# Modulation vectors of a two-block transformer: from TensorE products to VectorE multiply-and-sum

## The chip, the cores and the metric

The kernel runs on one core of one Trainium2 chip. The metric is the device time of one execution in microseconds (us); lower is better. PE is TensorE, DVE VectorE, ACT ScalarE, POOL GpSimd and SP SyncE, whose only work here is to issue DMAs.

## What is computed

Two transformer blocks of two layers each run one after the other on 1024 tokens of width 1024, in float32. In every layer a conditioning vector gives shifts, scales and gates, the modulation vectors:

```python
# first block, per layer: w_mod is 1024 x 3072
mod = silu(c) @ w_mod[l] + b_mod[l]                 # 24 vectors of 128
# second block, per layer: w_ada is 1024 x 6144, used for tokens and for context
mod_x = silu(c_2) @ w_ada[l] + b_ada[l]             # 48 vectors of 128
mod_c = silu(c_ctx_2) @ w_ada[l] + b_ada[l]
sh1, sc1, g1, sh2, sc2, g2 = split(mod_x, 6)
x = x + g1 * rmsnorm(mixer(rmsnorm(x, g) * (1 + sc1) + sh1), g_post)
x = x + g2 * rmsnorm(square(relu(hx2 @ w1)) @ w2, g_ff)
```

In blocks of 128 outputs that is 2 x (24 + 48) = 144 pieces of weight, 128 x 1024 numbers (512 KB) each. The first block's mixer joins window attention, retention and gated linear attention (GLA); the second block's joins window attention, a spatial gate and a Fourier transform, and a feed-forward follows it.

## The kernel before

**Stages.** `load_and_modulate` loads constants, computes the first layer's first 16 pieces and the rotation tables (to 57 us of the span). The first block follows, to about 1213 us, and then the second block, to the end at 3957 us.

**First block.** Four units (two layers, two halves of 512 tokens: unit 0 to 3), 283.2 us apart. A unit has 32 chunks; a chunk is one 128-wide slice of outputs: SP loads its weights into `wraw` (two slots, `load`), ACT copies them to `whi` (float32r, a rounded form), POOL subtracts to get the rest `wlo` (`split_low`, two halves), and PE makes 24 matmuls of 512 columns (`high_products`: `h_hi` and `h_lo` by `whi`; `low_products`: `h_hi` by `wlo`). Each chunk s of the first 24 is divided into two half-steps `at` = 2s and 2s + 1, and at each half-step every engine does its part of the mixer (`mixers(it, at)`), written out in tables of numbers: GLA's decays are summed at `at` 5 (DVE, `log_sums`), its seven levels are scored at `at` 8, 9, 10, 11, 12, 14 and 16 (`LEVEL_AT`), its outputs come at 19 to 22, retention's at 23 to 27, rotations of q and k at 2c + 3 for nine chunks c (`ROPE_AT`: 11, 13, 19, 21, ..., 31), attention from 30 on. No scheduler moves anything: each engine takes its instructions in the order written.

**A level.** POOL makes a distance (`distance`, L540), ACT takes its exponent, POOL multiplies keys (`keys`, L551) and DVE queries (`queries`, L922), PE scores (`level`, L1243) into `quad`, and DVE picks the wanted entries out of `quad` (`pick`, L932). PE scores level n + 1 only when level n is picked.

**Modulation.** In four units the remaining 128 pieces are computed, four in a group, 8 groups a unit. PE multiplies at chunks s with s % 4 < 2 (`mod_step`, matmuls at L189, two pieces each, into `bankM`); DVE transposes `bankM` (`mod_rows`, L1052); PE folds (`fold_products`, L197) at the chunks of `FOLD_AT`; DVE adds the bias (`mod_columns`, four instructions at L204). `bankM` also takes four sums over heads per unit (`head_sum`), so each user waits for the one before. `mod_ring` has four slots; SP loads two pieces at s % 4 = 1 and two at s % 4 = 2 (`mod_loads`, L500), behind the chunk's weights and, after rotated chunks, behind `turned_half`, four small DMAs (L491) that wait until ACT has copied out the chunk just finished.

**Unit edges.** A unit's last chunk is followed by the next one's first: DVE scales x (`x_scaled`, L863), adds the last bias group (L204), makes `h_lo` (`x_low`, L871), and then, when the root of the last squares is there, adds y to x (`update`, L890 and L891) ahead of the new unit's mixers.

**Second block.** 64 chunks per feed-forward of 512 tokens, in four groups of eight `hidden` and eight `output` chunks. In `hidden` DVE squares (L2551) and makes `a_lo` (L2554); in `output` it adds to y (L2577). The last layer's columns are made in `project` (`columns2`).

Of the kernel before, what the change touches and what calls it, by code (L numbers as in the profile page):

```python
# [17 lines left out]
P = 128  # L18
# [31 lines left out]
FOLD_AT = [4 * g + (2 if g in (3, 4) else 3) for g in range(8)]  # L50
# [10 lines left out]
MOD_RING = 4  # L61
# [11 lines left out]
ROW_PAD = 896  # L73
# [135 lines left out]
def load_and_modulate(nc, t, a, sem):  # L209

    groups = MOD_FIRST // MOD_GROUP
    with ExitStack() as ctx:
# [3 lines left out]
        ring = sb("first_ring", [P, MOD_FIRST, D])  # L216
# [18 lines left out]
        def _(sp):  # L235
            sp.dma_start(cvec[:], a["c"]).then_inc(vec_in, 16)
            sp.dma_start(t["fold"][:], a["fold"]).then_inc(vec_in, 16)
# [6 lines left out]
            for m in range(MOD_RING):  # L244
                sp.dma_start(t["mod_ring"][:, m, :], a["w_mod"][MOD_FIRST + m]).then_inc(t["mod_in"][m], 16)
# [4 lines left out]
            sp.wait_ge(t["rope_saved"], 16 * 4 * NB)  # L250

        @block.scalar
        def _(act):
# [10 lines left out]
            nc.scalar.activation(t["cact"][:, :, 0:VEC], cvec[:], ACT.Silu).then_inc(cact_ready, 1)  # L264
# [10 lines left out]
        def _(pe):  # L275
            def to_columns(g):
                pe.wait_ge(row_ready, g + 1)
                at = 4 * VEC * MOD_GROUP
                fold_products(nc, psM[:, at * g:at * (g + 1)], t["fold"][:], row[:, g % 2, :]).then_inc(turned, 1)

            pe.wait_ge(cact_ready, 2)
            for g in range(groups):
# [3 lines left out]
                for c in range(MOD_GROUP):  # L286
                    mod_products(nc, psR[g % 2], c * P, t["cact"], ring, g * MOD_GROUP + c).then_inc(summed, 1)
# [5 lines left out]
        def _(dve):  # L293
# [23 lines left out]
            nc.vector.memset(t["cact"][:], 0.0).then_inc(cact_ready, 1)  # L317
# [50 lines left out]
def first_block(nc, t, a, sem):  # L368

    with ExitStack() as ctx:  # L370
# [6 lines left out]
        mods, mod_ring, cact = t["mods"], t["mod_ring"], t["cact"]  # L377
# [12 lines left out]
        mod_row = sb("mod_row", [P, MOD_GROUP * P])  # L390
# [63 lines left out]
        mod_summed, mod_row_ready, mod_turned, mod_out = sig("mod_summed", MOD_GROUP), sig("mod_row_out", 1), sig("mod_turned", 1), sig("mod_out", 1)  # L454
        mod_in = t["mod_in"]
        mod_groups = (MODS - MOD_FIRST) // MOD_GROUP // UNITS
# [13 lines left out]
        def group_of(it, s):  # L470

            return it * mod_groups + s // 4

        def mod_source(m):
            return a["w_mod"][m] if m < DEPTH * MOD1 else a["w_ada"][m - DEPTH * MOD1]

        @block.sync
        def _(sp):
# [14 lines left out]
            def mod_loads(it, s):  # L493

                g = group_of(it, s) + 1
                for c in range(2 * (s % 4) - 2, 2 * (s % 4)):
                    m = MOD_FIRST + MOD_GROUP * g + c
                    if m < MODS:
                        sp.wait_ge(*mod_summed.after(g - 1, c + 1))
                        sp.dma_start(mod_ring[:, c, :], mod_source(m)).then_inc(mod_in[c], 16)  # L500

            sp.dma_start(rope[:], t["rope_tables"][0]).then_inc(rope_in.sem, 16)
            for c in range(2):
                load(0, c)
            for it in range(UNITS):
                for s in range(CH1):
# [3 lines left out]
                    if s % 4 in (1, 2):  # L510
                        mod_loads(it, s)
# [338 lines left out]
        def _(dve):  # L850
# [195 lines left out]
            def mod_rows(it, s):  # L1046

                g = group_of(it, s)
                dve.wait_ge(*mod_summed.after(g, MOD_GROUP))
                if g:  # L1050
                    dve.wait_ge(*mod_turned.after(g - 1, 1))
                nc.vector.transpose(mod_row[:], bankM[:]).then_inc(*mod_row_ready.one)  # L1052

            def mod_columns(it, s):

                g = group_of(it, s)
                q = MOD_FIRST + MOD_GROUP * g
                dve.wait_ge(*mod_turned.after(g, 1))
                biased(nc, mods[:, q:q + MOD_GROUP, :], bankM[:, 0:4 * VEC * MOD_GROUP], t["mod_bias"][:, q:q + MOD_GROUP],
                       MOD_GROUP).then_inc(*mod_out.one)  # L1060
                dve.wait_ge(*mod_out.after(g, 1))
# [2139 lines left out]
```

## Time and profile before

| | |
|---|---|
| time, median of 3 runs | 3964.49 us (3963.75 to 3964.65) |
| the profiled execution | 3959.07 us, span 3957.3 us |
| busy: PE, PE weight loads | 93%, 75% |
| busy: DVE, ACT, POOL | 54%, 44%, 45% |
| granted PE clock, mean | 0.976 of full speed |
| HBM read, whole run | 397.40 MB |

The profiled execution is 5.4 us faster than the median; 1.8 us of it lie outside its span. Busy shares are over stages with different limits; which engine sets the end of a stage is read from that stage's own rows. `mod_ring<-in_w_ada` stands for a DMA into `mod_ring`, `lin<-h_hi,whi` for a matmul of those two into PSUM.

### The profile page before, as it was taken

How to read it: one execution, taken by the hardware profiler on the slowest of the kernel's cores; microseconds unless marked ns; L12 is line 12 of the kernel's file. 1: busy time of each engine (PE TensorE's matmuls, PEld its weight loads, DVE VectorE, ACT ScalarE, POOL GpSimd, SP SyncE). 2: the span in 40 equal slices, each digit the busy share in tenths (PEclk: the TensorE clock that was granted, in tenths of full speed). 3: DMA queues.
4: the chain of work that ended last, by engine and by line, in shares of the span. 5: the costliest groups of instructions: out<-in, count | busy, mean ns of one | idle time of the engine just before them, and what ended most of it. 6: DMA issues, size and time to landing. Idle time of an engine off the chain costs nothing.

```text
span 3957.3 us, 61376 instructions
## 1 busy us (share of the span) xinstructions
PE 3674.5 (93%) x22388; PEld 2983.7 (75%) x22388; DVE 2127.4 (54%) x3355; ACT 1725.4 (44%) x2899; POOL 1775.3 (45%) x1288
## 2 busy tenths in 40 slices
PE   4999999999997899888999999999899899999997
PEld 3867767777776777667888998887777778888886
DVE  5546556556456567667224655336567674335234
ACT  2355355355354544555324453335454553243233
POOL 1543444344443422325445885555322355455454
PEclk8999999999999999999999999999999999999999
DMA  6433433433433321112232453222221122233323
GB/s 251 132 127 123 150 120 129 136 134 134 132 111 109 111 74 52 56 59 88 95 99 95 150 170 108 96 96 82 97 70 54 64 80 96 90 96 97 97 94 104
DMA packets 127221, 421.32 MB, mean 106 GB/s; under 512 B 17280, under 2 KB 19104, under 8 KB 126368
## 3 DMA queue, kind: packets, MB, share of 16 engines
q1 hardware_dynamic: 121488, 410.09, 31.2%
q10 hardware_dynamic: 5520, 8.34, 0.6%
q8 instruction: 140, 2.29, 0.2%
q14 instruction: 73, 0.60, 0.0%
HBM read 397.40 MB, written 6.29 MB: 102 GB/s over the span
## 4 chain that ended last, share of the span: by engine, by line
PE 54%; DVE 8%; ACT 3%; issue 2%; POOL 0%; DMA 0%; SPq 0%; ACTq 0%; DVEq 0%; POOLq 0%
PE lin L2673 30%; PE lin L2682 15%; PE bankO L2798 2%; PE lin L2931 2%; PE bankT L2740 2%; DVE x L2318 1%; DVE tmp L2284 1%; DVE y L2317 1%; DVE staged L2296 1%; PE scores L2773 1%; DVE h_lo L2307 1%; ACT whi L1903 1%; PE lin L2815 1%; PE scores L2774 0%; PE lin L2703 0%
## 5 line engine op out<-in xcount | busy, mean ns | idle before, releaser
L1884 POOL TENSOR_TENSOR wlo<-late_raw,whi 128x512 fp32r<-128x512 f32 x456 | 641.5, 1431 | 750.6 <-PE lin L2682 489.8
L1884 POOL TENSOR_TENSOR wlo<-wraw,whi 128x512 fp32r<-128x512 f32 x452 | 635.1, 1428 | 703.5 <-PE lin L2682 485.8
L2673 PE MATMUL lin<-h_hi,whi 128*128 128x512 f32 (+1 forms) x1896 | 709.3, 381 | 48.1 <-ACT y_context L2197 13.8
L2673 PE MATMUL lin<-h_lo,whi 128*128 128x512 f32 (+1 forms) x1896 | 695.9, 374 | 0.0
L525 POOL TENSOR_TENSOR wlo<-wraw,whi 128x512 fp32r<-128x512 f32 x260 | 356.7, 1393 | 465.9 <-PE lin L1170 284.6
L2673 PE MATMUL lin<-a_hi,whi 128*128 128x512 f32 (+1 forms) x1280 | 465.7, 371 | 10.9 <-ACT tmp L2206 8.1
L2673 PEld LDWEIGHTS lin<-h_hi,whi 128*128 128x128 f32 x1896 | 364.2, 192 | 132.3 <-issue 24.3
L2673 PE MATMUL lin<-a_lo,whi 128*128 128x512 f32 (+1 forms) x1280 | 462.6, 369 | 0.0
L1903 ACT ACTIVATE whi<-late_raw 128x1024 fp32r<-128x1024 f32 x228 | 239.2, 1058 | 509.0 <-PE lin L2673 406.8
L1903 ACT ACTIVATE whi<-wraw 128x1024 fp32r<-128x1024 f32 x226 | 237.3, 1058 | 487.1 <-PE lin L2673 402.9
L2682 PE MATMUL lin<-h_hi,wlo 128*128 128x512 f32 (+1 forms) x1896 | 440.4, 375 | 1.2 <-POOL wlo L1884 0.8
L2673 PEld LDWEIGHTS lin<-h_lo,whi 128*128 128x128 f32 x1896 | 364.8, 192 | 60.2 <-issue 1.2
L2682 PEld LDWEIGHTS lin<-h_hi,wlo 128*128 128x128 f32 x1896 | 335.3, 191 | 64.8 <-issue 4.4
L2551 DVE TENSOR_TENSOR tmp<-tmp 128x512 f32<-128x512 f32 (+1 forms) x160 | 185.2, 1157 | 333.8 <-ACT tmp L2206 328.2
L1162 PE MATMUL lin<-h_hi,whi 128*128 128x512 f32 x800 | 333.4, 417 | 13.1 <-DVE h_lo L871 13.1
L1162 PE MATMUL lin<-h_lo,whi 128*128 128x512 f32 x800 | 322.1, 403 | 0.0
L2682 PE MATMUL lin<-a_hi,wlo 128*128 128x512 f32 (+1 forms) x1280 | 288.6, 370 | 2.3 <-POOL wlo L1884 2.3
L2673 PEld LDWEIGHTS lin<-a_hi,whi 128*128 128x128 f32 x1280 | 242.3, 189 | 59.3 <-ACT tmp L2206 15.7
L2673 PEld LDWEIGHTS lin<-a_lo,whi 128*128 128x128 f32 x1280 | 242.4, 189 | 39.7 <-issue 0.2
L2577 DVE TENSOR_TENSOR y<-lin,y 128x512 f32 (+1 forms) x96 | 66.4, 692 | 361.3 <-PE lin L2682 361.0
L2682 PEld LDWEIGHTS lin<-a_hi,wlo 128*128 128x128 f32 x1280 | 224.8, 188 | 44.9 <-POOL wlo L1884 3.5
L622 ACT ACTIVATE whi<-wraw 128x1024 fp32r<-128x1024 f32 x130 | 136.7, 1057 | 269.1 <-PE lin L1162 200.7
(382 smaller groups left out, 6429.8 us busy)
## 6 DMA issues: line engine op xcount, KB each, us to landing
wraw<-in_w SPq DMA_DIRECT2D x332, 512.0 KB, 3.5
late_raw<-in_w SPq DMA_DIRECT2D x212, 512.0 KB, 3.4
mod_ring<-in_w_ada SPq DMA_DIRECT2D x96, 512.0 KB, 4.5
mod_ring<-in_w_mod SPq DMA_DIRECT2D x32, 512.0 KB, 4.6
tmp<-tmp SPq DMA_DIRECT2D x224, 64.0 KB, 2.0
first_ring<-in_w_mod SPq DMA_DIRECT2D x16, 512.0 KB, 16.6
wraw<-in_dft_tokens SPq DMA_DIRECT2D x16, 512.0 KB, 3.5
late_raw<-in_dft_tokens SPq DMA_DIRECT2D x16, 512.0 KB, 3.5
```

What stands on the lines that cost most here:

```text
L525: last = nc.gpsimd.tensor_tensor(wlo[:, s, half], wraw[:, s, half], whi[:, s, half].bitcast(F32), ALU.subtract)
L622: nc.scalar.activation(whi[:, s, :], wraw[:, s, :], ACT.Copy).then_inc(*w_hi.one)
L1162: last = nc.tensor.matmul(bank[c % 2], whi[:, c % 2, k * P:(k + 1) * P], h[:, k, :], start=(k == 0 and h is h_hi), stop=False)
L1884: last = nc.gpsimd.tensor_tensor(wlo[:, s, half], raw_chunk[r][:, half], whi[:, s, half].bitcast(F32), ALU.subtract)
L1903: nc.scalar.activation(whi[:, s, 0:D], raw_chunk[r], ACT.Copy).then_inc(*w_hi.one)
L2551: nc.vector.tensor_tensor(tmp[:, 2 + s, 0:w], tmp[:, 4 + s, 0:w], tmp[:, 4 + s, 0:w], ALU.mult).then_inc(*a_sq.one)
L2577: nc.vector.tensor_tensor(part, bank[s][:, 0:p.w], part, ALU.add).then_inc(*lin_free.one)
L2673: last = nc.tensor.matmul(bank[s][:, 0:p.w], whi[:, s, k * P:(k + 1) * P], h[:, k, 0:p.w], start=(k == 0 and h is parts[0]), stop=False)
L2682: last = nc.tensor.matmul(bank[s][:, 0:p.w], wlo[:, s, k * P:(k + 1) * P], parts[0][:, k, 0:p.w], start=False, stop=(k == KB - 1))
L2740: last = nc.tensor.transpose(out, probs[i % 2][:, kv, k * P:(k + 1) * P], ident[:])
L2798: last = nc.tensor.matmul(bankO[half, g * P:(g + 1) * P], v, probsT[:, kv, at:at + P], start=(k == 0), stop=(k == n - 1))
L2931: return nc.tensor.matmul(bank[c][:, 0:2 * P].rearrange("p (t n) -> p t n", t=2), x_part[:, k, cols], w[:, 0:2, k * P:(k + 1) * P], start= ...
```

## The change

The pieces from 16 on are laid out by output (a row of 1024 weights for each of 128 outputs, the partitions), in `mod_rows`. silu(c) of the three vectors is written to HBM (`c_flat`), and copied from there to all partitions (`c_wide`). One DVE instruction (`tensor_tensor_reduce`) then multiplies a piece by a vector, adds up along the row on top of the bias, and leaves the sum in `mods`. PE's `mod_step`, the fold, `mod_rows` and `mod_columns` are gone from the first block, and `head_sum` no longer waits for them. `w_ada` pieces need two products (tokens, context). In the first block each unit has 32 products at the half-steps of `MOD_AT`: 32 pieces of `w_mod` in unit 0 (one product each), 48 of `w_ada` (layer 0) in units 1 to 3 (two each). The other 48, of the last layer, go into the first layer's feed-forwards of tokens, 48 products in each of two. `mod_ring` has two slots; a slot's next load is issued by SP when the last product on it is done.

```diff
-FOLD_AT = [4 * g + (2 if g in (3, 4) else 3) for g in range(8)]
+MOD_AT = list(range(3, 30)) + [31, 35, 39, 43, 46]
-MOD_RING = 4
+MOD_RING = 2
...
+                for c in range(MOD_RING, MOD_EARLY):
+                    done = products_through(c - MOD_RING)
+                    if ((done - 1) // UNIT_MODS, MOD_AT[(done - 1) % UNIT_MODS] // 2 + 1) == (it, s):
+                        sp.wait_ge(*mod_done.after(0, done))
+                        sp.dma_start(mod_ring[:, c % MOD_RING, :], a["mod_rows"][c]).then_inc(mod_in[c % MOD_RING], 16)
...
+            def modulation(e):
+                c, v = mod_product(e)
+                row = mod_ring[:, c % MOD_RING, :]
+                if v < 2:
+                    dve.wait_ge(mod_in[c % MOD_RING], 16 * (c // MOD_RING + 1))
+                dve.wait_ge(wide_in[v % 2], 32 if v == 2 else 16)
+                if v == 1:
+                    dve.wait_ge(*mod_done.after(0, e))
+                nc.vector.tensor_tensor_reduce(row if v != 1 else mod_terms[:], row, c_wide[:, v % 2, :], 1.0,
+                                               t["mod_bias"][:, MOD_FIRST + c:MOD_FIRST + c + 1], ALU.mult, ALU.add,
+                                               mods[:, MOD_FIRST + c, v:v + 1]).then_inc(*mod_done.one)
...
             def mixers(it, at):
...
                 if at in ROPE_AT[:-1]:
                     rotate(it, ROPE_AT.index(at))
+                if at in MOD_AT:
+                    modulation(it * UNIT_MODS + MOD_AT.index(at))
...
             def head_sum(it, n):
                 pe.wait_ge(*head_sq_ready.after(it, n + 1))
-                if n in (0, 2):
-                    pe.wait_ge(*mod_out.after(it * mod_groups + HEAD_SUM_AT[n] // 8, 1))
-                else:
+                if it or n:
                     pe.wait_ge(*head_log.after(it, n))
...
                 for j in range(FF_CH):
                     hidden(g0 + j, p.ff_no * FF_GROUPS, j, j % 2, p.w)
+                    if modulating:
+                        modulation(j // 4, j // 2 % 2, j % 2)
...
+            def finish_modulation():
+                first, count = MOD_FIRST + MOD_EARLY, MOD2
+                dve.wait_ge(*late_mod_kept.after(MOD2, 0))
+                late = mods[:, first:first + count, 1:3]
+                link(nc.vector.tensor_tensor(late, late, ...))
+                columns2(nc, t, link, DEPTH - 1)
+                nc.vector.memset(keys_values[:], 0.0).then_inc(*keys_cleared.one)
```

In the feed-forwards `c_wide`, the terms and the pieces lie in tiles of the attention that are free by then (`keys_values`, `staged`), so `keys_values` is cleared again afterwards.

**DVE, unit 1, the levels.** L932 of before is L945 of after, L922 is L935, L1025 to L1027 are L1038 to L1040; a product is two ISA rows at L1068, the multiply and the write of its sum. Before:

```order
L922 TENSOR_TENSOR tmp<-gq,big 128x256
L932 COPY_PREDICATED big<-gla_mask,quad 128x128x8
L1025 TENSOR_TENSOR tmp<-tmp,rope 128x512
L1026 TENSOR_TENSOR tmp<-tmp,rope 128x512
L1027 TENSOR_TENSOR rq<-tmp 128x512
L1052 STREAM_TRANSPOSE mod_row<-bankM 128x512
L922 TENSOR_TENSOR tmp<-gq,big 128x256
L932 COPY_PREDICATED big<-gla_mask,quad 128x256x4
```

After, the same stretch:

```order
L935 TENSOR_TENSOR tmp<-gq,big 128x256
L945 COPY_PREDICATED big<-gla_mask,quad 128x128x8
L1038 TENSOR_TENSOR tmp<-tmp,rope 128x512
L1039 TENSOR_TENSOR tmp<-tmp,rope 128x512
L1040 TENSOR_TENSOR rq<-tmp 128x512
L1068 ISA mod_terms,mods<-mod_ring,c_wide,mod_bias 128x1024
L1068 ISA mods 128x1
L935 TENSOR_TENSOR tmp<-gq,big 128x256
L945 COPY_PREDICATED big<-gla_mask,quad 128x256x4
L1068 ISA mod_ring,mods<-mod_ring,c_wide,mod_bias 128x1024
L1068 ISA mods 128x1
```

A product stands behind every half-step's part, between one level's pick and the next level's queries; one transpose in eight half-steps is gone.

**DVE, unit 1, ahead of the decays' sums.** Before, behind `update`:

```order
L891 SCALAR_TENSOR_TENSOR x<-y,cols,x 128x512
L1052 STREAM_TRANSPOSE mod_row<-bankM 128x512
L898 TENSOR_SCALAR big<-big 128x512
L899 SCALAR_TENSOR_TENSOR big<-big 128x512
L902 SCALAR_TENSOR_TENSOR bsum<-ones,big 128x128 x4
```

After:

```order
L904 SCALAR_TENSOR_TENSOR x<-y,cols,x 128x512
L1068 ISA mod_terms,mods<-mod_ring,c_wide,mod_bias 128x1024
L1068 ISA mods 128x1
L1068 ISA mod_ring,mods<-mod_ring,c_wide,mod_bias 128x1024
L1068 ISA mods 128x1
L911 TENSOR_SCALAR big<-big 128x512
L912 SCALAR_TENSOR_TENSOR big<-big 128x512
L915 SCALAR_TENSOR_TENSOR bsum<-ones,big 128x128 x4
```

Two products now precede the sums that the levels start from.

## Rows read from the trace of the kernel before

**Rows 1.** The page, part 1: busy us, share of span, instructions.
```profile
PE 3674.5 (93%) x22388; PEld 2983.7 (75%) x22388; DVE 2127.4 (54%) x3355; ACT 1725.4 (44%) x2899; POOL 1775.3 (45%) x1288
```
**Rows 2.** Busy by stretch: stretch, length, PE, PEld, DVE, ACT, POOL, clock, DMA, GB/s.
```profile
485.00:505.00 20.00, 16.65 (x78) 12.11 (x82) 8.49 (x22) 8.53 (x18) 4.80 (x4) 0.91 0.40 132
```
**Rows 3.** Groups by shape, whole run: count, busy, mean ns, idle before.
```profile
L189 PE MATMUL bankM<-mod_ring,cact 128*32 128x128 f32 x2048 | 70.0, 278 | 14.1 <-DVE mods L204 8.2 <-issue 5.9
L197 PE MATMUL bankM<-mod_row,fold 128*128 128x48 f32 x64 | 11.1, 256 | 15.0 <-DVE mod_row L1052 15.0
```
**Rows 4.** Timeline of PE, unit 0: start, length, what, count, idle before it.
```profile
76.38 0.76 PE L1162 MATMUL lin<-h_hi,whi 128*128 128x512 f32 x1 [9.00 <-DVE h_lo L871]
...
117.66 1.08 PE L189 MATMUL bankM<-mod_ring,cact 128*32 128x128 f32 x32
118.67 1.12 PE L1243 MATMUL quad<-tmp,big 32*128 32x64 f32 x32
```
**Rows 5.** Waits within unit 1 (334 to 617 us): us in total, times, longest.
```profile
PE bankM L197 <- DVE mod_row L1052: 3.7, 2, 2.9
```
**Rows 6.** Timeline of DVE, edge of units 0 and 1.
```profile
346.63 7.48 DVE L863 SCALAR_TENSOR_TENSOR big<-x,cols,tmp 128x512 f32<-128x512 f32 x8 [2.28 <-ACT tmp L634]
```
**Rows 7.** Timeline of PE, unit 1: the first and the last of seven levels.
```profile
392.92 1.12 PE L1243 MATMUL quad<-tmp,big 32*128 32x64 f32 x32
...
425.65 1.12 PE L1243 MATMUL quad<-tmp,big 32*128 32x64 f32 x32
```
**Rows 8.** Timeline of DVE, unit 1, `update`'s end to the levels.
```profile
381.80 0.68 DVE L890 TENSOR_TENSOR y<-y,rstd 128x512 f32<-128x512 f32 x1
...
386.37 2.27 DVE L908 TENSOR_TENSOR big<-quad,ident 128x2048 f32<-128x2048 f32 x1
...
402.44 0.42 DVE L922 TENSOR_TENSOR tmp<-gq,big 128x256 f32<-128x256 f32 x1 [1.78 <-ACT big L674]
403.10 1.30 DVE L932 COPY_PREDICATED big<-gla_mask,quad 128x1024 f32<-128x1024 uint8 x1 [0.24 <-PE quad L1243]
...
409.81 0.69 DVE L1026 TENSOR_TENSOR tmp<-tmp,rope 128x512 f32<-128x512 f32 x1
410.54 1.21 DVE L1027 TENSOR_TENSOR rq<-tmp 128x512 f32<-128x512 f32 x1
...
419.24 2.48 DVE L932 COPY_PREDICATED big<-gla_mask,quad 128x1024 f32<-128x1024 uint8 x1
```
**Rows 9.** Timeline of POOL, unit 1, the levels.
```profile
394.88 0.74 POOL L551 TENSOR_TENSOR big<-gk,big 128x256 f32<-128x256 f32 x1
...
396.62 2.52 POOL L525 TENSOR_TENSOR wlo<-wraw,whi 128x512 fp32r<-128x512 f32 x2
...
403.40 1.04 POOL L540 TENSOR_TENSOR big<-bsum 128x512 f32<-128x512 f32 x1
...
410.22 0.98 POOL L551 TENSOR_TENSOR big<-gk,big 128x256 f32<-128x256 f32 x1 [1.41 <-ACT big L674]
```
**Rows 10.** DVE, like operations: a timeline row; ns min/median/max of the reducing form.
```profile
22.45 1.22 DVE L305 SCALAR_TENSOR_TENSOR y<-tmp,y 128x1024 f32<-128x1024 f32 x1
...
L2344 DVE CUSTOM_DVE_ANT_0 scores<-scores,mask_band,mx x128: 619/625/628, 1362.8 to 3120.4; 128x384 f32<-128x384 f32 x128
L2344 DVE DVE_READ_ACCUMULATOR2_ANT mx<- x128: 140/143/145, 1363.3 to 3121.0; 128x1 f32 x128
...
L983 DVE CUSTOM_DVE_ANT_0 quad<-quad,mask x128: 406/465/469, 213.4 to 1133.5; 128x256 f32<-128x256 f32 x128
```
**Rows 11.** Timeline of SP, unit 1, chunk 5; below, landing of L500's DMAs.
```profile
402.91 2.42 SPq L491 DMA_DIRECT2D tmp<-tmp  x4
405.38 1.08 SPq L500 DMA_DIRECT2D mod_ring<-in_w_ada  x2
...
DMA to landing us min/median/max: 3.4/4.5/6.9
```
**Rows 12.** Timeline of DVE, feed-forward, one hidden chunk.
```profile
1930.00 1.14 DVE L2551 TENSOR_TENSOR tmp<-tmp 128x512 f32<-128x512 f32 x1 [2.61 <-ACT tmp L2206]
```

More of the change, by code:

```diff
@@ L250, in _ @@
             sp.wait_ge(t["rope_saved"], 16 * 4 * NB)
+            sp.wait_ge(t["c_saved"], 16)
         @block.scalar
@@ L504, in _ @@
                 load(0, c)
+            for v in range(2):
+                sp.dma_start(c_wide[:, v, :], t["c_flat"][v:v + 1].partition_broadcast(P)).then_inc(wide_in[v], 16)
             for it in range(UNITS):
@@ L1863, in _ @@
                 for b in FF_ROWS[l]:
-                    run(ff_at(l, b), l, IN2 + KB, FF2)
+                    if l == 0 and b < NB:
+                        run_with_modulation(ff_at(l, b), l, IN2 + KB, b)
+                    else:
+                        run(ff_at(l, b), l, IN2 + KB, FF2)
             for s in range(2):
@@ L2391, in project @@
                             attended(l, s - 2)
-                        if p.in_no == 0 and s == 4:
-                            columns2(nc, t, link, DEPTH - 1)
                         if p.b == 0 and 1 <= s < 4:
@@ L2563, in feed_forward, with outputs, modulation @@
                 later = pre_mix(l + 1, 0) if nxt and nxt.rows.l > l else None
-                def outputs(g, first):
-                    with dve.Fori(0, FF_CH // 2) as i:
-                        for s in range(2):
-                            output(g + (2 * i + (FF_CH + s)), s,
-                                   product_rows(p)[:, bass.ds(2 * i + s, 1), 0:p.w].rearrange("p o n -> p (o n)"), first)
+                modulating = l == 0 and not p.context
+                def outputs(g, first, pairs):
+                    with dve.Fori(0, FF_CH // 4) as i:
+                        for s in range(4):
+                            output(g + (4 * i + (FF_CH + s)), s % 2,
+                                   product_rows(p)[:, bass.ds(4 * i + s, 1), 0:p.w].rearrange("p o n -> p (o n)"), first)
+                            if modulating and pairs is not None:
+                                modulation(pairs + i, s // 2, s % 2)
+                def modulation(pairs, r, v):
+                    row, c = mod_ring[:, r, :], 2 * pairs + (MOD_LATE * p.b + r)
+                    sums = mod_sums[:, r, v:v + 1]
+                    if v == 0:
+                        dve.wait_ge(*late_wide_in.after(0, 32))
+                        dve.wait_ge(*late_mod_in[r].after(pairs + MOD_LATE // 2 * p.b, 16))
+                    ins = nc.vector.tensor_tensor_reduce(row if v else mod_terms, row, c_wide[:, v, :], 1.0, 0.0, ALU.mult, ALU.add, sums)
+                    if v:
+                        ins.then_inc(*late_mod_done.one)
+                        dve.wait_ge(*late_mod_done.after(c, 1))
+                        m = MOD_FIRST + MOD_EARLY
+                        place = mods[:, c + m:c + m + 1, 1:3] if isinstance(c, int) else mods[:, bass.ds(c + m, 1), 1:3]
+                        nc.vector.tensor_copy(place, mod_sums[:, r:r + 1, :]).then_inc(*late_mod_kept.one)
                 def output(gi, s, part, first):
@@ L2602, in feed_forward @@
                         add_square("pre", nxt, j, pre_sums(nxt))
+                    if modulating and p.b == NB - 1 and j == 3:
+                        finish_modulation()
                 for k in range(KB):
```

194 lines of the change are left out of this document (109 added, 85 removed).

## The prediction, made before the run

> **What bounds the kernel now.** I read three views in order. The page's busy shares [rows 1] say PE 93%, DVE 54%: PE is what the kernel is made of, and the question is where it would wait. The groups of the modulation's lines [rows 3] give what PE does for it: 2048 small matmuls, busy 70.0 us in all, and 64 small ones of the fold, 11.1 us, with 14.1 and 15.0 us of idle time ahead of them. All of it lies in the first block. The timeline then shows whether this is on the path: in the first block PE goes from one matmul to the next with hardly a gap (the modulation's own waits are most of the idle time of a unit), so a microsecond taken from PE is a microsecond of time, until another engine is late. The other engines' room has to be read where the new work is put: half-steps 3 to 29, of which 8 to 16 hold GLA's levels [rows 7 to 9].
>
> **What goes from PE.** A modulation step at one chunk takes 117.66 to 118.67, start to start [rows 4]: 1.01 us. 16 steps a unit: 16.2. A fold is 11.1 / 32 = 0.35 busy [rows 3], less 0.08 that overlaps as in the step: 0.27, 8 a unit: 2.2. Waits of the shared bank, from the same rows: 15.0 / 4 for the transpose and 5.9 / 4, 5.2 us inside a unit, and 8.2 / 3 = 2.7 at each of three edges. After the longest, 2.9 us [rows 5], PE's granted clock is 0.91 over 20 us instead of full [rows 2], some 1.5 us (0.09 x 20, a little less): that comes back too. The edge does not: its 2.7 us wait is replaced. `x_scaled` runs 7.48 us [rows 6] from a root that hangs on PE two chunks back, then `x_low` follows; before it goes only the 0.7 us of bias adding. PE's first step of the unit (1.01) goes, and it waits for `h_lo` instead: the gain there is 0.7, not 3.7. Sum for a unit: 16.2 - 1.0 + 0.7 + 2.2 + 5.2 + 1.5 = 24.8, less 0.3 for the last fold, that lies in the replaced wait: **24.5 us**. Four units would give 98.
>
> **What a product costs DVE.** No row has it. Nearest below: 128x1024 float32 from two SBUF tiles, 1.22 us, and the write of an accumulator 0.14 [rows 10]: 1.37. Above: the two reducing forms there give 0.406 to 0.465 us at 256 elements and 0.625 at 384; the steepest pair is 1.71 ns an element, so 1024 take at most 1.72, with the write 1.86. I take 1.37, since the flat pair (1.25 ns) is closer to it, and its own waits beside.
>
> **Where the products meet POOL.** L1027 takes 1.21 us at 410.54, right on POOL's L551 of 410.22 to 411.20; the like L1026 just before, with POOL idle, takes 0.69 [rows 8, 9]. So a DVE operation on two SBUF tiles stood still until POOL's ended. The Trainium skill (SBUF — State Buffer, section SBUF: two separate sides) has this as a rule that speaks against the change: DVE and GpSimd share a port pair, an exclusive lock for the whole instruction when DVE reads two SBUF inputs. The trace agrees, 1.21 against 0.69; without that rule the sum would be the first rival's.
>
> I count such time for unit 1's levels, from the end of the decays' sums to level 6. Before, `update` ends at 382.5 [rows 8]; now 0.7 earlier, then two products (2.7) and the sums (383.9, where the transpose behind `update` ends, to 386.37: 2.45 [rows 8]): POOL can start at 387.0. From there POOL has 8 distances of 1.04, 7 keys of 0.74 and 4 chunks' splits of 2.52 [rows 9]: 23.6. DVE's two-tile operations are 7 queries of 0.42, two rotations of 3 x 0.69 [rows 8], and ten products (half-steps 5 to 14) of 1.23: 19.4. Together 43.0, one after the other: 430.0. With the last pick but one (2.48 [rows 8]), which comes behind, and handovers, level 6 starts at **433**. Before it started at 425.65 [rows 7], and with the gains up to there (0.7, four steps, two folds: 5.3) it would be 420.4. So **12.6 us** of the unit's 24.5 are lost. From below: if only DVE's own queue counted (12 products 16.4, picks 9.0, sums, diagonal, queries and rotations 11.7, from 381.8) it would be done at 418.9, no loss. From above, at 1.86 a product, 12 x 0.49 = 5.9 more. I take the port sum, as POOL's row at 410.22 (0.98 for 0.74) shows the lock hitting both ways already now.
>
> After the levels (17 to 29) 13 products lie between state updates, with 8 or 16 large matmuls of PE between its own parts; I take 1 us lost, between 0 and 4. In attention there are five, with room. Units 1 to 3: 24.5 - 12.6 - 1 = **10.9 each, 32.7**.
>
> **Unit 0** differs three times. Its first step is hidden already (PE waits 9.00 us right behind it for the first `h_lo` [rows 4]): -1.0. There is no `update`, so the two early products are free: +2.7 on the level part (9.9 lost). But each of its products needs a piece of its own. SP issues the pieces for 2s and 2s + 1 only behind the four small DMAs, which wait for the end of chunk s - 1 and take 2.42 us; the pieces follow, 2.5 us behind the first of them, and land 3.4 to 6.9 us later, median 4.5 [rows 11]: 7 us or more into chunk s. DVE wants them at 2s, stands still, and behind it in its queue stands the state update for which PE waits. Followed through chunks 9 to 15 with those lengths PE loses 1.7 us at chunk 9, 0.6 at 12 and some 4.5 at the first scores: -6.8 (0 to -25, if every landing takes 6.9). In units 1 to 3 a piece serves two products and is needed behind the rotation, so it has landed. Unit 0: 24.5 - 1.0 - 9.9 - 6.8 - 1 = **5.8**.
>
> **Second block.** In a hidden chunk DVE idles 2.61 us [rows 12], POOL having finished by then; a product (1.37, with the copy of two sums now and then 0.2) fits: 0. In each of the two feed-forwards' first group hidden 4 to 7 also carry two updates, DVE is full, and 4 products come on top; what is then late is `a_lo` of the last chunk, for which PE waits: 2 us each, **-4** (0 to -8). `finish_modulation` is some 5 us on DVE over four hidden chunks with 1.3 us free each: **-1**. SP's new waits come behind four loaded chunks: 0. Pieces move 64 MB as before. The start is bound by DVE's rotation arguments, which stay: 0. `columns2` leaves `project`: 0.
>
> **Sum.** 32.7 + 5.8 - 4 - 1 = **33.5 us** off 3959.07 of the profiled execution: 3925.6; off the median, 5.4 above it: 3931.0.
>
> **Rivals.** (a) *The lock hardly counts*: product and POOL interlock in the idle time that both have (POOL waits 1.41 us for ACT before L551 [rows 9]). Level part 2 instead of 12.6, 9.9; unit 0 loses nothing to landings either: 3 x 21.5 + 20.5 - 1 = 84, median 3880. For it: POOL is busy only 45% [rows 1]. Against: the port sum fills the stretch. (b) *Nothing is left*: a product is 1.86. Units 1 to 3: 10.9 - 5.9 - 1 = 4, unit 0: 5.8 - 8 = -2, second block -6: 4 us, 3960, no change. (c) *Slower*: a product runs at half rate on DVE, 2.3 + 0.14. Then 12 x 1.07 = 12.8 more in each level part and 3 more between state updates: units 1 to 3 -4.9 each, unit 0 -10; in a hidden chunk the product fills the 2.61 us, and the first groups lose 5 more each: 3964.5 + 14.7 + 10 + 15 = 4004. It decides from about 1.9 us a product. Against: no reducing row is near 2.2 ns an element. The same side is reached if the chain of levels needs more handovers than I counted. That the products are not made is excluded by the order of instructions.
>
> **Chances.** Forecast (gain 10 to 60) 0.50; (a) 0.17; (b) 0.15; (c) 0.18. A measurement of this kernel tells about 0.2%, 8 us, from no change: faster 0.68, same 0.13, slower 0.19. The range goes from (a)'s 3880 to 3985, which leaves the far part of (c) out; the forecast's own range is 3905 to 3955.
>
> **What would show it.** Right: no L189 matmul in the first block past 57 us; products of 1.37 to 1.9 us; unit spacing 283.2 down to some 272; level 6 some 40 us behind level 0 (now 32.7), with PE gaps of 2 to 4 us on `lq` or a pick; POOL's operations there near 1.5 us; unit 0 the longest of the four. Wrong: spacing near 262, or above 283; products over 2 us; PE waiting for `wlo` or for ACT's copies instead; gaps of several us in the feed-forwards.

## The result, and the profile after

The changed kernel takes 3971.4 us (median of 11 runs, 3969.2 to 3977.7), the kernel before 3964.2 (11 runs, 3960.1 to 3965.2): a ratio of 1.0022, 95% interval 1.0013 to 1.0030. It is slower by 7 us between the medians and by 9 in the ratio, where 33.5 us less were forecast. In the profiled executions the span goes from 3957.3 to 3967.4. Of the experiments below, one execution of b1_half_attention took 15755 us at a granted clock of 0.66, and is left out of its numbers.

The page of the changed kernel, part 1 (busy us, share of span, instructions), answers to [rows 1]:

```profile
PE 3624.3 (91%) x20276; PEld 2935.2 (74%) x20276; DVE 2476.4 (62%) x3692; ACT 1724.6 (43%) x2900; POOL 1883.3 (47%) x1288
```

PE is busy 50 us less and the kernel is longer all the same. DVE has 349 us more work, and POOL 108 us more, though it has as many instructions as before. The starts of the five sums over x (L1228 before, L1236 after) in the timelines of PE cut the run into units:

| us of the span | unit 0 | unit 1 | unit 2 | unit 3 | last sum to the span's end |
|---|---|---|---|---|---|
| before | 271.6 | 283.2 | 283.3 | 283.3 | 2772.6 |
| after | 275.6 | 279.3 | 280.0 | 281.8 | 2786.8 |
| forecast for after | 265.8 | 272.3 | 272.4 | 272.4 | 2777.6 |

So units 1 to 3 gain 8.6 us instead of 32.7, unit 0 loses 4.0 instead of gaining 5.8, and the part behind the fourth unit is 14.2 longer instead of 5. The products themselves came out as forecast. By line, DVE's L1068 in the first block (ns min/median/max; the second row is the write of a sum's place):

```profile
L1068 DVE DVE_READ_ACCUMULATOR2_ANT mods<- x128: 75/78/92, 83.4 to 1139.9; 128x1 f32 x128
L1068 DVE CUSTOM_DVE_ANT_0 mod_ring<-mod_ring,c_wide,mod_bias x80: 1253/1286/2547, 82.2 to 1138.1; 128x1024 f32<-128x1024 f32 x80
L1068 DVE CUSTOM_DVE_ANT_0 mod_terms<-mod_ring,c_wide,mod_bias x48: 1256/1750/2560, 386.8 to 1129.3; 128x1024 f32<-128x1024 f32 x48
```

1.25 us alone and 0.08 for the sum: 1.33, where 1.37 was taken. Up to 2.56 beside POOL.

**One unit.** The balance of unit 1 is one row of busy time by stretch (stretch, length, then busy us of PE, PE's weight loads, DVE, ACT, POOL, then granted clock, DMA share, GB/s). Before:

```profile
335.00:618.20 283.20, 270.05 (x2043) 208.33 (x2039) 158.67 (x293) 132.38 (x246) 123.56 (x94) 0.98 0.38 132
```

After:

```profile
339.40:618.70 279.30, 254.35 (x1511) 194.71 (x1511) 205.30 (x313) 132.00 (x245) 137.70 (x93) 0.97 0.32 104
```

As an estimate, half of such a time is lost where PE multiplies: 3.4 us more, which is why the busy time fell by 15.7 and not by the 18.9 of the short products below. Its waits in unit 1 (us in total, times, longest), before:

```profile
PE bankM L197 <- DVE mod_row L1052: 3.7, 2, 2.9
PE bankM L189 <- DVE mods L204: 2.7, 1, 2.7
PE lin L1196 <- DVE h_lo L1043: 2.3, 2, 1.3
PE bankM L189 <- issue: 1.5, 2, 0.7
PE lin L1162 <- DVE h_lo L871: 1.3, 2, 0.7
PE bankE L1382 <- ACT av L754: 0.7, 1, 0.7
PE bankM L1337 <- ACT tmp L645: 0.6, 1, 0.6
```

After:

```profile
PE lin L1170 <- DVE h_lo L884: 4.6, 3, 3.2
PE bankM L1343 <- ACT tmp L658: 3.9, 1, 3.9
PE quad L1251 <- POOL big L564: 3.3, 1, 3.3
PE lin L1204 <- DVE h_lo L1056: 3.2, 2, 2.3
PE quad L1372 <- POOL big L580: 2.9, 2, 1.5
PE bankE L1388 <- ACT av L767: 1.7, 1, 1.7
PE quad L1358 <- ACT esink L717: 1.6, 1, 1.6
```

The three lines of the shared bank (L197, L189) are gone, 7.9 us, and seven others are new or longer. The prediction had reckoned with a wait in the place of the first and with later sums in the place of the third.

**The longest new one** is in attention, where it had counted nothing. DVE after, around the first scores, which PE makes at 496.24 (start, length, what):

```profile
492.13 2.20 DVE L1068 CUSTOM_DVE_ANT_0 mod_terms<-mod_ring,c_wide,mod_bias 128x1024 f32<-128x1024 f32 x1
...
494.27 1.27 DVE L1068 CUSTOM_DVE_ANT_0 mod_ring<-mod_ring,c_wide,mod_bias 128x1024 f32<-128x1024 f32 x1
...
496.08 1.75 DVE L1039 TENSOR_TENSOR tmp<-tmp,rope 128x512 f32<-128x512 f32 x1
497.86 1.67 DVE L1040 TENSOR_TENSOR aq<-tmp 128x512 f32<-128x512 f32 x1
499.56 1.28 DVE L1068 CUSTOM_DVE_ANT_0 mod_terms<-mod_ring,c_wide,mod_bias 128x1024 f32<-128x1024 f32 x1
...
500.77 0.43 DVE L996 CUSTOM_DVE_ANT_0 quad<-quad,mask 128x256 f32<-128x256 f32 x1
```

ACT after, the same place, and below it PE:

```profile
502.83 0.47 ACT L715 ACTIVATE big<-quad,nmax 128x256 f32<-128x256 f32 x1 [6.58 <-DVE sink_arg L1002]
...
506.17 0.60 ACT L658 ACTIVATE tmp<-bankM 128x512 f32<-128x512 f32 x1
```
```profile
506.91 0.67 PE L1343 MATMUL bankM<-tmp,ones 128*128 128x512 f32 x1 [3.87 <-ACT tmp L658]
```

Before, scores made at 495.31 had their maximum at 496.60 (an idle DVE waited for them) and the exponents at 498.66, and PE waited 0.64. Now the maximum (L996) stands behind three products and a rotation. The first product is stretched by POOL's `wlo` of 490.14, and two of the rotation's operations by that of 495.60. Counted from the scores it begins 3.2 us later (4.5 instead of 1.3); the exponents follow, then the logarithm of the sum over heads, which stands behind them in ACT's queue, and PE waits for that. The two long waits of PE in this unit, ended at 397.53 and 506.91, are followed by the lower clock, from 398.3 for 6.8 us and from 507.5 for 3.4. The first of the two stretches:

```profile
398.20:405.20 7.00, 5.83 (x29) 4.57 (x25) 4.15 (x6) 3.44 (x6) 6.56 (x6) 0.51 0.41 138
```

### The profile page after: what moved, and what is told of

The parts are those of the page before. It is cut to its first block, busy times and chain, and to the rows that moved or that the text cites. A ratio compares the mean times of both kernels' runs of the same rounds, so it can differ in the third digit from the quotient of the medians.

```text
span 3967.4 us, 57554 instructions
## 1 busy us (share of the span) xinstructions
PE 3624.3 (91%) x20276; PEld 2935.2 (74%) x20276; DVE 2476.4 (62%) x3692; ACT 1724.6 (43%) x2900; POOL 1883.3 (47%) x1288
## 4 chain that ended last, share of the span: by engine, by line
PE 52%; DVE 9%; ACT 3%; issue 2%; POOL 0%; DMA 0%; SPq 0%; ACTq 0%; DVEq 0%; POOLq 0%
PE lin L2749 29%; PE lin L2758 14%; PE bankO L2874 2%; PE lin L3007 2%; PE bankT L2816 2%; DVE tmp L2328 1%; DVE a_lo L2596 1%; PE lin L2891 1%; DVE x L2362 1%; DVE staged L2340 1%; PE scores L2849 1%; DVE h_lo L2351 1%; DVE y L2361 1%; DVE tmp L2593 1%; ACT whi L1945 1%
## 5 line engine op out<-in xcount | busy, mean ns | idle before, releaser
L1926 POOL TENSOR_TENSOR wlo<-late_raw,whi 128x512 fp32r<-128x512 f32 x456 | 668.3, 1489 | 742.6 <-PE lin L2758 478.4
L1926 POOL TENSOR_TENSOR wlo<-wraw,whi 128x512 fp32r<-128x512 f32 x452 | 661.3, 1487 | 672.6 <-PE lin L2758 451.6
L538 POOL TENSOR_TENSOR wlo<-wraw,whi 128x512 fp32r<-128x512 f32 x260 | 388.4, 1515 | 392.5 <-PE lin L1178 215.8
L2749 PE MATMUL lin<-a_hi,whi 128*128 128x512 f32 (+1 forms) x1280 | 466.0, 371 | 12.7 <-ACT tmp L2250 8.3
L1945 ACT ACTIVATE whi<-wraw 128x1024 fp32r<-128x1024 f32 x226 | 237.3, 1058 | 487.4 <-PE lin L2749 350.0
L2596 DVE TENSOR_TENSOR a_lo<-tmp,a_hi 128x512 fp32r<-128x512 f32 (+3 forms) x160 | 230.3, 1439 | 15.5 <-DVE tmp L2593 12.7
```

Of the source, the lines that this page charges most:

```text
L538: last = nc.gpsimd.tensor_tensor(wlo[:, s, half], wraw[:, s, half], whi[:, s, half].bitcast(F32), ALU.subtract)
L1926: last = nc.gpsimd.tensor_tensor(wlo[:, s, half], raw_chunk[r][:, half], whi[:, s, half].bitcast(F32), ALU.subtract)
L1945: nc.scalar.activation(whi[:, s, 0:D], raw_chunk[r], ACT.Copy).then_inc(*w_hi.one)
L2596: nc.vector.tensor_tensor(a_lo[:, unit, 0:w].rearrange("p o n -> p (o n)"), tmp[:, 2 + s, 0:w], a_hi[:, unit, 0:w].rearrange("p o n -> p ( ...
L2749: last = nc.tensor.matmul(bank[s][:, 0:p.w], whi[:, s, k * P:(k + 1) * P], h[:, k, 0:p.w], start=(k == 0 and h is parts[0]), stop=False)
```

## The experiments

Theory A: the products did it; PE's removed work comes back in full once DVE is free. Theory B: a part of PE's removed work was never on the path alone: chains through DVE, ACT and POOL are about as long, and PE only waits where it multiplied before.

**Short products everywhere, and in the first block alone.** In `modulation` of both blocks, and for the second kernel of the first block alone (the vectors are then wrong, and the order of instructions stays):

```diff
-                nc.vector.tensor_tensor_reduce(row if v != 1 else mod_terms[:], row, c_wide[:, v % 2, :], 1.0,
+                n = 8
+                nc.vector.tensor_tensor_reduce(row[:, 0:n] if v != 1 else mod_terms[:, 0:n], row[:, 0:n], c_wide[:, v % 2, 0:n], 1.0,
```

> The changed kernel, each product cut from 1024 columns to 8, in both blocks (so the modulation vectors are not computed); every wait, load and instruction stays. Theory A (DVE's time for the products is what was lost, on the levels and ahead of the first scores): nearly all of PE's removed work shows, 80 to 90 us off before: 3875 to 3885 us. Theory B (PE's modulation steps were cover for chains of softmax and level handovers that are as long without them): the first block gets only half of it back, 3915 to 3930. If the second block's 10 us more of the changed kernel come from the feed-forwards' products, its end lies as far behind the first block's end as before; if from the layout of SBUF or the waits, 7 to 10 us of them stay.

> The changed kernel with the first block's products cut to 8 columns and the feed-forwards' 96 left whole (the first block's vectors are not computed). Against e1_short_all this prices the feed-forwards' products. If they cost what the gaps at a_lo show: 3 us more than e1_short_all. If they cause all of the second block's loss: 10 us more.

Measured: 3917.2 and 3922.0 us (ratios 0.9880, 0.9866 to 0.9895, and 0.9888, 0.9874 to 0.9902). That is B: with products that cost next to nothing the change is worth 47 us and not 98. Unit 1 of e1_short_all:

```profile
329.80:598.20 268.40, 251.19 (x1512) 193.44 (x1511) 168.02 (x313) 132.05 (x245) 124.38 (x93) 0.98 0.33 108
```

Against before, PE is busy 18.9 us less (270.05 - 251.19), which is the forecast's steps and folds, 18.4, and the lower clock is granted for 10.2 us in both. But PE is idle 17.2 us instead of 13.2: 14.8 us gained, not 24.5. Its waits:

```profile
PE lin L1171 <- DVE h_lo L884: 4.6, 3, 3.2
PE quad L1373 <- POOL big L580: 3.2, 2, 1.6
PE lin L1205 <- DVE h_lo L1056: 2.6, 2, 2.3
PE bankM L1344 <- ACT tmp L658: 1.7, 1, 1.7
PE bankE L1389 <- ACT av L767: 1.7, 1, 1.7
PE lin L1171 <- ACT gv L783: 1.4, 1, 1.4
```

POOL's normalising (L580), ACT's copy of values (L767) and the head sum's logarithm (L658) are links of attention's chain, none of them touched by the change. The step of PE that stood between a score and the next link is gone, and PE waits for the link instead. The second kernel's 5 us more lie within the spread of its runs (3914.7 to 3924.3), and fit the 3 us of the feed-forwards' products.

**Short products beside the levels alone.** `n = 8 if MOD_AT[e % UNIT_MODS] <= 16 else D`.

> The changed kernel with only the products of half-steps 3 to 16 cut to 8 columns (those vectors are not computed). By the prediction's ledger the products there cost 12.6 us in three units and 9.9 in the first, 48 in all: 3923. By the offsets of the two traces (3.3 us behind at level 6 where 5.3 ahead were due) some 8 a unit: 3938. If theory B holds and the levels only wait for each other, 3960.

3946.2 us (0.9955, 0.9942 to 0.9968): 25 us less than the changed kernel. Units 272.8, 273.0, 271.9, 275.6. In unit 1 the products to half-step 16 cost 6.3 us (279.3 - 273.0) and those behind 4.6 (273.0 - 268.4). The ledger had 12.6 and 1. The lower clock is granted for 17.1, 13.7 and 10.2 us in the three, so some 1.7 us of either price is clock.

**Half of PE's modulation in attention; half of it elsewhere; twice of it in attention.** Three kernels made from the one before; the first two, which compute wrong vectors:

```diff
-def mod_products(nc, bank, at, cact, ring, slot):
-    for k in range(KB):
+def mod_products(nc, bank, at, cact, ring, slot, short=False):
+    for k in range(4 if short else KB):
...
-                                start=(k < 4), stop=(k >= 4))
+                                start=(k < 4), stop=(short or k >= 4))
...
-                        mod_products(nc, bankM, c * P, cact, mod_ring, c).then_inc(*mod_summed.one)
+                        mod_products(nc, bankM, c * P, cact, mod_ring, c, 15 <= s < OUT1).then_inc(*mod_summed.one)
```

The second has `not 15 <= s < OUT1`. The third calls `mod_products` twice where `15 <= s < OUT1`.

> The kernel before, with half of PE's matmuls taken out of the modulation steps of chunks 16, 17, 20 and 21 (beside attention), so those vectors are wrong; all waits stay. Each step is 0.5 us shorter, 16 steps: 8 us. Theory A: PE sets the pace here too, 8 us faster, 3956. Theory B: the softmax chain is as long without, 0 to 3 us faster, 3961 to 3964.

> The kernel before, with half of PE's matmuls taken out of the modulation steps everywhere but at chunks 16, 17, 20 and 21 (so those vectors are wrong): 12 steps of a unit 0.5 us shorter. If PE sets the pace outside attention: 6 us a unit, 24 us faster, 3940. If the levels and the chains at the end of the unit also take some of it back, as the 15 of 24.5 us in e1_short_all say: 3944 to 3950.

> The kernel before, with PE's modulation matmuls of chunks 16, 17, 20 and 21 done twice over (the second pass gives the same sums): 4 us more PE work in a unit, 16 in all. If PE's steps in attention are cover for the softmax chain there is no such cover left unused (PE idles 13 us a unit in all): a step of 1 us more is partly hidden, 4 to 10 us slower, 3967 to 3973. If PE sets the pace there: 16 us slower, 3979. Together with b1_half_attention, which took 2 us a unit away and left the units at 283.3, it says how far the cover reaches.

b1_half_attention takes 3960.3 us (0.9990, 0.9981 to 0.9999), b2_half_rest 3955.1 (0.9970, 0.9959 to 0.9982), b3_twice_attention 3974.7 (1.0033, 1.0021 to 1.0045). The kernel before, timed beside them, has medians of 3964.0, 3962.9 and 3962.4. So 3.7 us come back of 8 taken away in attention, 8 to 12 (median, ratio) of 24 taken away elsewhere, and 12 are lost for 16 added. No part of PE's work is worth its full length, and the timed runs do not set attention apart; b2_half_rest came out above both of its expectations.

In the profiles, a unit without 2 us in attention is 283.3 us long, as before; without 6 us elsewhere 279.9; with 4 us more in attention again 283.2 or 283.3. That does not mean that it all went into waits. PE's idle time in unit 1 is 13.2 us before, 13.1 with half and 12.7 with twice, while the lower clock is granted for 10.2, 13.7 and 0 us. The stretch that holds the four steps, from the first maximum of the scores (L983) to L1035, has no lower clock in any of the three: 77.9 us before, 77.5 with 2 us less work, 80.7 with 4 us more, and within 0.1 us the same in units 2 and 3. So attention by itself gave back 0.5 of 2 us and charged 2.8 of 4. For taking away that is B: a quarter comes back. For adding it holds in part only. The rest of what the whole units show is clock and small waits at the unit's edge. Stretch 460 to 500, before, then with half, then with twice (columns as above):

```profile
460.00:500.00 40.00, 37.07 (x258) 27.96 (x251) 20.78 (x45) 10.39 (x21) 12.88 (x10) 0.96 0.37 120
```
```profile
460.00:500.00 40.00, 37.07 (x242) 27.75 (x234) 20.40 (x43) 9.12 (x17) 12.90 (x10) 0.91 0.37 120
```
```profile
460.00:500.00 40.00, 37.07 (x264) 27.81 (x263) 22.40 (x47) 10.39 (x20) 12.87 (x10) 1.00 0.38 120
```

The same busy and idle time, but a granted clock of 0.96, 0.91 and 1.00: over 40 us some 1.6 us lost before, 3.6 with less work, 0 with more (the third kernel's unit starts 2.9 us later, so its stretch lies as much earlier in the unit). All three have the wait of 2.9 us for the transpose there.

**The same number of products, other places.**

```diff
-MOD_AT = list(range(3, 30)) + [31, 35, 39, 43, 46]
+MOD_AT = list(range(5, 28)) + [30, 32, 34, 36, 38, 40, 42, 44, 46]
```

> The changed kernel with nine of a unit's 32 products moved: none at half-steps 3 and 4 (ahead of the decays' sums), none at 28, 29, 31, 35, 39 and 43; instead one at each even half-step from 30 to 44, right behind the maximum of the scores, while ACT takes the exponents. Against the changed kernel at 3971: if the place of a product decides (3.0 us a unit read at the decays' sums, 3.8 in attention, about 1 given back at the new places), 20 to 25 us faster, 3947 to 3951. If a product costs its time wherever it stands, 3971.

3945.5 us (0.9955, 0.9942 to 0.9969), nothing left out: 26 us faster than the change and 17 faster than before (3962.9 beside it). By the two lists eight products a unit moved, not nine: those of half-steps 3, 4, 28, 29, 31, 35, 39 and 43. Units 273.4, 272.3, 273.8, 274.3. PE's wait for the head sum's logarithm in unit 1, 3.9 us after the change:

```profile
PE bankM L1343 <- ACT tmp L658: 0.6, 1, 0.6
```

So the account of the longest wait holds: the product in front of the maximum cost it, and the same product behind the maximum, while ACT takes exponents, costs nothing that this wait shows. Of the 7.0 us that unit 1 gained, level 6 had 1.1; most lies behind it. How much belongs to the two early products and how much to the six others was not tried apart.

**Only the last layer's pieces on DVE.** The first block as before, five groups a unit instead of eight; 48 pieces as products in the feed-forwards. The core of the edit to the kernel before (with it the second block's part of the change):

```diff
-FOLD_AT = [4 * g + (2 if g in (3, 4) else 3) for g in range(8)]
+MOD_BLOCKS = [1, 2, 4, 5, 6]
+FOLD_AT = [4 * g + (2 if g in (3, 4) else 3) for g in MOD_BLOCKS]
...
             def mod_step(it, s):
+                if s // 4 not in MOD_BLOCKS:
+                    return
```

> The first block as before on PE, but with five groups a unit instead of eight (those of chunks 0 to 3, 12 to 15 and 28 to 31 are gone); only the last layer's 48 pieces are products on DVE, in the feed-forwards as in the change. By the offsets of e1_short_all those three places gave 1.6, 4.4 and 3.7 us a unit: 39 in all, less 4 for the feed-forwards' products and 4 to 6 that the second block lost beside them: 3929 to 3935. If what is taken from PE is given back by the chains behind it, as in attention: 3950 to 3960.

3928.8 us (0.9915, 0.9901 to 0.9929), the fastest version that leaves nothing out: 34 us less than before (3962.9 beside it), 43 less than the change. Units 261.9, 271.7, 272.4, 272.7. Unit 1:

```profile
325.60:597.30 271.70, 260.96 (x1842) 201.37 (x1841) 155.44 (x277) 132.38 (x245) 123.95 (x93) 0.99 0.34 114
```

PE is busy 9.1 us less than before, some 1.7 of it clock (6.8 us at the lower level instead of 10.2), and its idle time has fallen too, to 10.7: 11.5 us gained. The wait of 2.9 us for the transpose has gone with its group. The groups left lie beside the levels and attention; that those three are worth the most was read from e1_short_all, and no run takes other groups away.

**The first unit's loads.** In v1_even, for `it == 0`, `mod_loads(it, s)` stands ahead of `turned_half` in SP's queue.

> v1_even (3945.5) with one more edit: in the first unit SP issues the pieces of a chunk ahead of the four small DMAs of the rotation instead of behind them, so some 2.5 us earlier. The prediction put 6.8 us of the first unit down to late pieces. In the changed kernel DVE stands still for a piece 9 times, 28 us, in the first unit, and the unit gained 5.6 us with short products where the others gained 15. If the place in SP's queue is the cause: 3 to 7 us faster than v1_even, 3939 to 3942. If the pieces are late because a slot comes free only one chunk ahead: no change, 3945.

3949.5 us (0.9965, 0.9952 to 0.9979), no gain on v1_even's 3945.5 (the runs of the two overlap); unit 0 is 275.1 instead of 273.4. DVE's waits in unit 0, of v1_even:

```profile
DVE mod_ring L1068 <- DMA mod_ring<-in_mod_rows: 18.3, 6, 5.5
```

Of v2_loads_first:

```profile
DVE tmp L1041 <- DMA tmp<-tmp: 11.6, 5, 5.6
...
DVE mod_ring L1071 <- DMA mod_ring<-in_mod_rows: 9.6, 3, 5.6
```

The waits for pieces are halved as meant, and DVE waits for the rotation's small DMAs instead, which are now behind the pieces: 21.2 us in all. One wait took the other's place.

**Products out of the levels and into the output chunks.** `MOD_AT = [5, 6, 7] + list(range(13, 28)) + list(range(30, 57, 2))`, with a call in the loop over the output chunks.

> v1_even (3945.5) with five of the nine products that lie beside the levels (half-steps 8 to 12) moved to the output chunks 24 to 28, one a chunk. The offsets of v1_even against e1_short_all put some 4.5 us a unit on the twelve products from the decays' sums to the last level, and DVE idles 2 us or more in each output chunk. If the levels' part pays for each product: 2 us a unit, 8 us faster, 3937. If DVE's delay is given back only where the whole stretch is free, or the output chunks wait for DVE's h_lo then: 3943 to 3948.

3955.1 us (0.9980, 0.9971 to 0.9989), 10 slower than v1_even and outside of both expectations. PE's waits in unit 1:

```profile
PE quad L1240 <- DVE tmp L869: 3.1, 1, 3.1
...
PE bankE L1279 <- ACT khT L695: 2.2, 1, 2.2
```

Neither is in v1_even's unit 1 at this size (it has none for L869 and 0.3 for khT). The first is the sum over x at the unit's edge, whose squares DVE adds up in the chunks that the products went to; idle time of 2 us in a chunk wasn't room, since the chain through DVE ran in it. The second is ahead of GLA's output; why it appears when the products move out of the levels was not tried apart. Beside both the clock falls, at 335.4 and 441.2: unit 1 has 20.5 us at the lower level where v1_even has 13.7, an estimated 3.4 of the 4.9 us that it is longer.

**Both kernels, profiled again.**

> The kernel before, unchanged, profiled a second time. In the first profile the second block runs 2753.2 us from the first block's last sum to the end; in b1_half_attention and b2_half_rest, which leave the second block alone, 2757.7 and 2762.0. If the first profile was a short one: 2756 to 2762 here. If the second block is always that long: 2753, and the changed kernel's 2767.4 is 14 us worse.

> The changed kernel, unchanged, profiled a second time. Units of 279 to 282 us again in either case. Second block 2767 if the extra belongs to the change; 2760 to 2764 if half of it was the one execution.

3964.5 and 3967.7 us. Units 1 to 3 are within 0.6 us of the first profiles; unit 0 of the changed kernel is 279.4 instead of 275.6. The part behind the last sum, over all profiles, and below each row the time in it at the lower clock:

| | us |
|---|---|
| kernels with the second block as before (before, c1, b1, b2, b3) | 2772.6, 2778.5, 2776.8, 2781.1, 2778.9 |
| of it at 0.50 | 118.2, 134.5, 134.5, 134.4, 134.4 |
| with whole products in the feed-forwards (after, c2, e2, e3, v1, v2, v3) | 2786.8, 2781.5, 2789.6, 2782.5, 2786.5, 2786.2, 2789.0 |
| of it at 0.50 | 142.1, 133.5, 142.2, 134.5, 141.5, 137.8, 133.4 |
| with short ones (e1) | 2785.7 |
| of it at 0.50 | 144.4 |
| as after, first block on PE (h1) | 2778.3 |
| of it at 0.50 | 130.8 |

The first profile of before was the shortest of its kind, 6 below the others' mean, and had 16 us less at the lower clock. The means of the two kinds are 2777.6 and 2786.0, 8.4 apart. Less half of the time at the lower clock, an estimate of what the full clock would leave, they are 2712.0 and 2717.1, with e1 at 2713.4 and h1 at 2712.9.

## Why the prediction was wrong

**What goes from PE: this is the step that failed.** "Sum for a unit ... 24.5 us" was measured at 14.8 (e1_short_all). The work in it, 18.4, was right (18.9). What did not come are the 5.2 us of shared-bank waits and the 1.5 of clock: PE's idle time rose by 4.0 us, and the lower clock was granted for 10.2 us as before. Both had gone in as pure gain, because "a microsecond taken from PE is a microsecond of time, until another engine is late". The prediction then looked for a late engine only where it put products. In attention the engines were already just in time: before, PE waited 0.64 for the head sum, 0.7 for values, nothing for normalised scores. Short waits like these, one after another, mean a chain about as long as PE's work, not room. b1_half_attention shows it by itself: 2 us less work, 0.5 us back across attention. Over four units these 9.7 us would be 39, more than the whole forecast gain.

**Half-steps 17 to 29 and attention.** "I take 1 us" and "In attention there are five, with room" were 4.6 us together (e3_short_levels against e1_short_all), among them 3.9 of waiting for one logarithm against 1.7 with short products, and some 1.7 of clock. DVE's share there was low, but a product was put ahead of the maximum, on the way from score to exponent. v1_even moved six of these and the two ahead of the decays' sums, and regained 26 us.

**The levels.** 12.6 us were forecast and 6.3 measured (both with the first two products), so the port sum was too dear by half. That the engines get in each other's way is there. POOL in the stretch of the levels of unit 1, by shape (count, busy, mean ns, idle before), before:

```profile
L540 POOL TENSOR_TENSOR big<-bsum 128x512 f32<-128x512 f32 x8 | 9.3, 1169 | 5.2 <-DVE bsum L902 5.2
L551 POOL TENSOR_TENSOR big<-gk,big 128x256 f32<-128x256 f32 x7 | 6.1, 873 | 4.5 <-ACT big L674 4.5
```

After:

```profile
L553 POOL TENSOR_TENSOR big<-bsum 128x512 f32<-128x512 f32 x8 | 11.0, 1376 | 8.4 <-DVE bsum L915 8.4
L564 POOL TENSOR_TENSOR big<-gk,big 128x256 f32<-128x256 f32 x7 | 8.2, 1177 | 4.5 <-ACT big L687 4.5
```

The means rise by 0.2 and 0.3 us. This is what the Trainium skill (SBUF — State Buffer, section SBUF: two separate sides) says of the shared port pair, and 108 us more of POOL's busy time with the same instructions agree. But the prediction laid all of both engines' work end to end, and that was not the path. PE's first and last level after:

```profile
397.53 1.34 PE L1251 MATMUL quad<-tmp,big 32*128 32x64 f32 x32 [3.34 <-POOL big L564]
...
433.42 1.12 PE L1251 MATMUL quad<-tmp,big 32*128 32x64 f32 x32
```

35.9 us apart, 32.7 before [rows 7], forecast "some 40". Levels in unit 1, us from the unit's start:

| | level 0 | level 1 | level 6 |
|---|---|---|---|
| before | 57.9 | 62.8 | 90.6 |
| e1_short_all | 55.4 | 61.8 | 88.4 |
| after | 58.1 | 66.8 | 94.0 |
| v1_even | 55.7 | 63.7 | 92.8 |

Against short products the change loses 5.6 us up to level 6. 2.7 are lost ahead of level 0, in the wait of 3.34 for the sums behind two products; v1_even, with none there, has it at 55.7. 2.3 more are lost from level 0 to level 1, just where the clock is at its lower level for 6.8 us, worth an estimated 3.4; in e1_short_all there is none in unit 1, and 3.4 us of it at this place in unit 2 make that step 8.0 us instead of 6.4. From level 1 to level 6, with six products between and the full clock, the change takes 27.2 us, short products 26.6 and the kernel before 27.8. Sharing with POOL, which was to cost most of the 12.6, costs some 0.6 there, and 2.6 in v1_even, where PE waits 2.0 for `wlo`.

**Unit 0.** Forecast 5.8 gained, measured 4.0 and 8.5 lost (the two profiles). Late pieces were the right cause in kind: in the changed kernel DVE waits 20.6 us for them in this unit, six times (the 28 us of the expectation above are the whole block's). With short products this unit gains 5.5 where unit 1 gains 14.8, so 9.3 us go there and not 7.8 (6.8, and 1.0 for the first step). But not all of it is waiting: the lower clock is granted in this unit for 17.6 us before, 28.8 with short products, and 30.6 and 41.3 in the two profiles of the change, an estimated 5.6 of the 9.3, and more than the 3.8 by which the two profiles differ. That the pieces had "landed" in units 1 to 3 was nearly so: DVE waits 7.5 us for them there, three times in all. That they are late because of their place in SP's queue was only half right (v2_loads_first).

**Second block.** -5 forecast. In the feed-forwards PE's waits grow as forecast. Between 1840 and 2757, the three that differ, before:

```profile
PE lin L2703 <- DVE h_lo L2307: 4.7, 3, 2.2
PE lin L2682 <- POOL wlo L1884: 2.3, 6, 0.9
PE lin L2673 <- DVE a_lo L2554: 1.5, 1, 1.5
```

After:

```profile
PE lin L2779 <- DVE h_lo L2351: 6.1, 3, 3.7
...
PE lin L2749 <- DVE a_lo L2596: 3.1, 3, 1.5
PE lin L2758 <- POOL wlo L1926: 2.6, 6, 0.9
```

1.4, 1.6 and 0.3: 3.3 us, and the two first groups have their gap at `a_lo`. The rest of the 14.2 us is not the products': e1_short_all has it too. It is clock: this part has 118.2 us at the lower level in the first profile of before and 142.1 in that of the change, half of which is 12.0; e1_short_all's 144.4 against 118.2 are its whole 13.1. Why the clock is granted so differently in stages whose instructions didn't change stays open.

**The sum.** In unit 1 the forecast was 7.0 us too good: 9.7 on PE's side and 3.6 behind the levels, less 6.3 charged too much beside them; in units 1 to 3 together 24.1, in unit 0 9.8, in the last part 9.2, which the clock more than covers. The clock is inside the other terms too: 1.5 us a unit were to come back, and unit 1 has 6.8 us more at the lower level, some 3.4 lost. In the medians the change loses 7 and not 10. Of the rivals, (b), nothing left at 3960, came nearest in time, but not by its reason: products were 1.33 us and not 1.86. Rival (c) had the side right, and its last sentence, that the levels' chain might need more handovers, was the right kind of thought in the wrong place.

## What to carry to other kernels

An engine that is busy 93% with hardly a gap does not yet set the time alone. Before an engine's work is counted as gain, follow for each place the chain through the other engines that ends in the next wait of that engine, and count only the difference; a row of waits of 0.6 us suggests that it is near zero. The cheapest test is to halve that work where it stands, and to read the result together with the granted clock: here an unchanged unit was in part waits and in part clock.

When work is moved to an engine with idle time, its place in the order matters more than its length: not ahead of an operation for which another engine waits, better right behind it. The same 32 products a unit cost 3971 or 3945 us by their place. And work can be taken away in part: here three groups of eight gave 34 us, where all eight gave none. And idle time that two engines share is no reason to add up their work end to end: find which operations the waiting engine waits for.

## What was not expected of the hardware

- Multiplying two 128x1024 float32 tiles and adding up along the row takes DVE 1.25 us alone, 1.22 ns an element, and 0.08 for the sum's place; the like form in attention wrote its place in 0.14 [rows 10].
- The granted clock of TensorE gave back part of what was changed in its work: 0.96, 0.91 and 1.00 over the same 40 us with the same idle time, and 10.2, 13.7 and 0 us at the lower level in the unit, for the work as it was, 2 us less and 4 us more. In unit 1 of before and after, PE had waited 2.7 to 3.9 us shortly before each fall; the kernel with 4 us more has waits of 2.7 and 2.9 there and no fall. What decides was not tried.
- Two profiles of one kernel differ by up to 6 us behind the first block with the same instructions (2772.6 and 2778.5), with 118.2 and 134.5 us at the lower clock. A difference of that size in one stage of one profile is no evidence before the clock of that stage has been compared.
